# Opening of a residual block kernel on one core: column transposes spread and moved, a third product mixed in, VectorE's angle work and the small loads reordered

## The reference

```python
def rmsnorm(x, gain):
    xf = x.astype(jnp.float32)
    y = xf * lax.rsqrt(jnp.mean(xf * xf, axis=-1, keepdims=True) + RMS_EPS)
    return (y * gain.astype(jnp.float32)).astype(x.dtype)
...
    mod = jax.nn.silu(c) @ w_ada + b_ada
    shift, scale, gate = jnp.split(mod, 3, axis=-1)
    h = rmsnorm(x, norm_pre) * (1.0 + scale[:, None, :]) + shift[:, None, :]
    proj = h @ w_in
    u_pool, z_pool, u_ssm, z_ssm, g_pool, g_ssm = jnp.split(proj, list(IN_SPLITS), axis=-1)
...
    dt = jnp.exp(log_dt.astype(jnp.float32))[:, None]
    lam_re = jnp.minimum(a_re.astype(jnp.float32), -1e-4)
    mag = jnp.exp(lam_re * dt)
    abar_re = mag * jnp.cos(lam_im * dt)
    abar_im = mag * jnp.sin(lam_im * dt)
```

## Time and profile before

| | us |
|---|---|
| median of 3 runs | 974.56 (974.37 to 975.2) |
| the profiled execution, its time | 974.84 |
| the profiled execution, its span in the trace | 973.0 |
| TensorE busy (PE) | 942.2, 97% of the span |
| VectorE busy (DVE) | 650.1, 67% |
| ScalarE busy (ACT) | 345.2, 35% |
| GpSimd busy (POOL) | 46.6, 5% |

### The profile page before, as it was taken

How to read it: one execution, slowest core, us unless ns; L and a number is a source line. 1 busy time by engine, 2 the same in 40 slices (tenths; PEclk the granted TensorE clock), 3 DMA queues, 4 the chain that set the end, 5 groups by cost and what they waited for, 6 DMA issues and landing times.

```text
span 973.0 us, 11601 instructions
## 1 busy us (share of the span) xinstructions
PE 942.2 (97%) x4448; PEld 790.3 (81%) x4448; DVE 650.1 (67%) x912; ACT 345.2 (35%) x401; POOL 46.6 (5%) x82
## 2 busy tenths in 40 slices
PE   0999999999999999999999999999999999999997
PEld 0878888888888888888888888888888888787886
DVE  6968978999888868767887667663344444455233
ACT  6541342322443343644554544631122231133111
POOL 0019800000000000000000000000000000000000
PEclk9999999999999999999999999999999999999999
DMA  9833273544445569667566554897543255322222
GB/s 339 298 113 105 90 262 131 190 155 152 152 160 188 187 204 238 207 180 207 172 187 210 157 155 125 265 334 239 173 154 109 105 201 210 129 87 87 87 87 86
DMA packets 95686, 168.26 MB, mean 173 GB/s; under 512 B 37648, under 2 KB 54160, under 8 KB 95632
## 3 DMA queue, kind: packets, MB, share of 16 engines
q1 hardware_dynamic: 86272, 163.07, 50.1%
q10 hardware_dynamic: 9360, 4.46, 2.1%
HBM read 118.21 MB, written 49.28 MB: 172 GB/s over the span
## 4 chain that ended last, share of the span: by engine, by line
PE 91%; DVE 5%; ACT 2%; DMA 1%; issue 1%; SPq 0%; ACTq 0%; DVEq 0%
PE ps L1791 52%; PE ps L1879 17%; PE ps L1979 8%; PE psb L1879 4%; PE ps L1925 2%; PE psa L1900 1%; PE psa L1848 1%; PE psa L1791 1%; PE psb L1914 1%; PE psb L1912 1%; DMA sin_t<-yp_d 1%; PE psb L1815 1%; DVE mod_out L1268 0%; ACT gt L980 0%; DVE w_lo L1264 0%
## 5 line engine op out<-in xcount | busy, mean ns | idle before, releaser
L1791 PE MATMUL ps<-bop,w_hi 128*128 128x512 f32 x1312 | 352.7, 391 | 0.5 <-DVE bop L1302 0.3
L1791 PEld LDWEIGHTS ps<-bop,w_hi 128*128 128x128 f32 x1312 | 245.2, 188 | 51.6 <-DVE bop L1656 0.6
L1791 PE MATMUL ps<-bop,w_lo 128*128 128x512 f32 x656 | 202.0, 389 | 0.0
L1791 PEld LDWEIGHTS ps<-bop,w_lo 128*128 128x128 f32 x656 | 123.2, 188 | 25.7
L1264 DVE TENSOR_TENSOR w_lo<-raw,w_hi 128x1024 fp32r<-128x1024 f32 x49 | 61.4, 1254 | 59.8 <-ACT w_hi L968 59.7
L968 ACT ACTIVATE w_hi<-raw 128x1024 fp32r<-128x1024 f32 x49 | 51.6, 1057 | 91.8 <-PE ps L1791 84.4
L1879 PE MATMUL ps<-bop,r_hi 128*128 128x512 f32 x208 | 64.1, 390 | 0.0
L1879 PE MATMUL ps<-t_hi,r_hi 128*128 128x512 f32 x140 | 55.2, 395 | 0.0
L1879 PE MATMUL ps<-t_hi,r_lo 128*128 128x512 f32 x140 | 54.6, 390 | 0.0
L1879 PE MATMUL ps<-t_lo,r_hi 128*128 128x512 f32 x140 | 54.5, 389 | 0.0
L1979 PE MATMUL ps<-wo_hi,y_hi 128*128 128x512 f32 x128 | 49.9, 390 | 0.4 <-DVE wo_lo L1721 0.4
(11 more groups left out here) (304 smaller groups left out, 1515.6 us busy)
## 6 DMA issues: line engine op xcount, KB each, us to landing
raw<-in_wstream SPq DMA_DIRECT2D x58, 512.0 KB, 5.4
pair_raw<-in_wstream SPq DMA_DIRECT2D x22, 512.0 KB, 4.7
ada<-in_w_ada SPq DMA_DIRECT2D x16, 512.0 KB, 11.6
x_tok<-in_x SPq DMA_DIRECT2D x8, 512.0 KB, 7.7
gs_d<-gt SPq DMA_DIRECT2D x8, 512.0 KB, 5.0
win_d<-win_new SPq DMA_DIRECT2D x8, 512.0 KB, 4.0
wout_d<-wout_new SPq DMA_DIRECT2D x8, 512.0 KB, 5.6
wout<-wout_d SPq DMA_DIRECT2D x8, 512.0 KB, 4.2
```

The costliest lines, as they stand in the source:

```text
L1791: last = mm(ps[slot(u)][:, f * HALF:f * HALF + HALF], a[:, k, :], b(k, f), start=k == 0 and q == 0, stop=k == KT - 1 and q == 2)
```

## The change

It has four parts, all in the opening.

- **Loads.** ScalarE's queue issues ldt, aim, cols, are and consts; SyncE's starts with x, with c behind tile 3. The first two weight blocks are loaded behind w_ada of k = 0 and k = 1.
- **Row sums.** VectorE takes the squares of tiles 2 and 5 (`square_sum`), ScalarE the other six. `plain_angles` stands ahead of VectorE's first square sum and `reduced_angles` behind it, both ahead of the first scales of x. `sine` and a new function `cosine` (the first part of the old `cos_sin`) move behind the loop over k, ahead of split_lo(3); what is left of `cos_sin` stands behind it. split_lo(0), (1) and (2) stand inside the loop, split_lo(4) moves ahead of `magnitudes`.
- **Transposes.** Columns 0 to 3 are transposed into four PSUM tiles ahead of all products, tokens of the first four x tiles first, as soon as each diagonal exists. ScalarE copies columns 2 to 7 out of PSUM (`xt_out`) and makes h from the copy. Column k + 4 is transposed behind the k steps of k.
- **Third product.** Its k steps stand among those of the first two: k = 0, 1 behind k = 5, then 2, 3 behind 6, the rest behind 7. `split_hi(2)` waits for the last transpose.

```diff
+        xt = [ps[0], ps[1]] + [psb, psa] * 3
...
             for t in range(CH):
                 sp.dma_start(x_tok[:, t, :], x_view[t]).then_inc(tile_in[t], 16)
-            load_w(0)
-            load_w(1)
+                if t == 3:
+                    sp.dma_start(silu_row[:, :], c_d).then_inc(c_in, 16)
             for k in range(KT):
+                if k in (1, 2):
+                    load_w(k - 1)
...
+            act.dma_start(par["ldt"], log_dt_d).then_inc(par_in, 16)
+            act.dma_start(par["aim"], a_im_d).then_inc(par_in, 16)
+            act.dma_start(cols[:, :], cols_d).then_inc(cols_in, 16)
+            act.dma_start(par["are"], a_re_d).then_inc(par_in, 16)
+            act.dma_start(consts[:, :], consts_d).then_inc(small_in, 16)
...
+            def xt_out(k):
+
                 act.wait_ge(xt_done, k + 1)
+                fn(h_full[k][:, :], xt[k][:, :], ACT.Copy).then_inc(xt_taken, 1)
...
+            split_hi(0)
+            h_of(0)
+            h_high(0)
+            xt_out(2)
+            split_hi(1)
+            h_of(1)
+            xt_out(3)
+            h_high(1)
+            for k in range(2, KT):
+                h_of(k)
+                h_high(k)
+                if k + 2 < KT:
+                    xt_out(k + 2)
+                if k == 5:
+                    split_hi(2)
...
+            def square_sum(t):
+                dve.wait_ge(tile_in[t], 16)
+                stt(rt[1][:, :], x_tok[:, t, :], 1.0, x_tok[:, t, :], ALU.mult, ALU.mult,
+                    accum_out=stat[:, 0, t:t + 1]).then_inc(v_sums, 1)
...
                 scale_shift(k)
                 if k:
                     split_h(k - 1)
+                if k < 2:
+                    split_lo(k)
+                if k == 6:
+                    split_lo(2)
             split_h(KT - 1)
-            split_lo(2)
+            sine(steps)
+            cosine(steps)
+            split_lo(3)
             cos_sin(steps)
-            split_lo(3)
+            split_lo(4)
             magnitudes(steps)
             dve.wait_ge(angle_ready, 1)
             factors(steps)
-            split_lo(4)
             complex_factor(steps)
...
+            for tiles in (range(0, 4), range(4, CH)):
+                for k in range(4):
+                    transposed(k, tiles)
+            third = {5: (0, 1), 6: (2, 3), 7: (4, 5, 6, 7)}
             for k in range(KT):
-                if k + 2 < KT:
-                    x_transposed(k + 2)
-                pe.wait_ge(h_done, k + 1)
-                for n in range(2):
-                    last = k_step(("gs", n), k, *h)
-                    if k == KT - 1:
-                        last.then_inc(mm_done, 1)
-            for u in FIRST[2:]:
+                step(0, k)
+                step(1, k)
+                for k3 in third.get(k, ()):
+                    step(2, k3)
+                if k + 4 < KT:
+                    transposed(k + 4, range(CH))
+            for u in FIRST[3:]:
                 product(u, h)
```

More of the change, by code:

```diff
@@ L550, in sine, with cosine @@
             do(stt(wide["sn"], p, 1.0, r, ALU.add, ALU.mult))
-        def cos_sin(steps):
+        def cosine(steps):
             do = steps.do
@@ L568, in cos_sin @@
             do(tt(q, q, p, ALU.mult))
+        def cos_sin(steps):
+            do = steps.do
+            tt = nc.vector.tensor_tensor
+            k, q, z = (wide[m] for m in ("k", "q", "z"))
+            cs, sn = wide["cw"], wide["sw2"]
             do(tt(cs, k, wide["cs"], ALU.mult))
@@ L965, in split_hi @@
                 act.wait_ge(raw_in[p % 2], 16 * (p // 2) + 16)
-                if previous(p) is not None:
+                if p == 2:
+                    act.wait_ge(xt_done, KT)
+                elif previous(p) is not None:
                     act.wait_ge(mm_done, previous(p) + 1)
                 fn((wx_hi if p == 2 else w_hi[p % 2])[:, :, :], raw[p % 2][:, :, :], ACT.Copy).then_inc(hi_done, 1)
[L970 to L976, removed]
-                    act.wait_ge(tile_in[t], 16)
-                    if t:
-                        act.wait_ge(x_sums, t)
-                    fn(gt[t % 2][:, :], x_tok[:, t, :], ACT.Square, accum_out=stat[:, 0, t:t + 1]).then_inc(x_sums, 1)
+            act.dma_start(par["ldt"], log_dt_d).then_inc(par_in, 16)
[3 more added lines that the diff above has]
+            act.dma_start(consts[:, :], consts_d).then_inc(small_in, 16)
+            act.wait_ge(cols_in, 16)
+            fn(stat[:, 5, 0:1], cols[:, 0:1], ACT.Silu)
+            done = 0
+            for half_, tiles in enumerate(X_TILES_ACT):
+                for t in tiles:
+                    act.wait_ge(tile_in[t], 16)
+                    if done:
+                        act.wait_ge(x_sums, done)
+                    fn(gt[done % 2][:, :], x_tok[:, t, :], ACT.Square, accum_out=stat[:, 0, t:t + 1]).then_inc(x_sums, 1)
+                    done += 1
+                if half_ == 0:
+                    act.wait_ge(c_in, 16)
+                    fn(silu_row[:, :], silu_row[:, :], ACT.Silu).then_inc(silu_ready, 1)
                 act.wait_ge(x_var, half_ + 1)
@@ L1282, in _ @@
                 if half_ == 0:
-                    sine(steps)
-            split_lo(0)
-            split_lo(1)
-            dve.wait_ge(silu_ready, 1)
-            do(ts(g_col[:, :], b_ada[:, KT:2 * KT], 1.0, None, ALU.add))
+                    dve.wait_ge(silu_ready, 1)
+                    dve.wait_ge(cols_in, 16)
+                    do(ts(g_col[:, :], b_ada[:, KT:2 * KT], 1.0, None, ALU.add))
             def scale_shift(k):
```

75 lines of the change are left out of this document (46 added, 29 removed).

## The result

The changed kernel took **980.38 us** in the median of five runs (979.11 to 980.92), the kernel before 974.83 in the five beside them (974.37 to 975.37): a ratio of 1.0053, 95% interval 1.0038 to 1.0068. It is slower, where 970.3 was forecast. The profiled execution took 979.22 us (span 977.4).

The account below looks back on a forecast made before the run. TensorE's chain of matmuls was taken to bound the kernel. 1.8 us won at the first product plus 3.0 up to the fourth, less 0.5 of later waits, made 4.3: 974.56 - 4.3 = 970.3 us, range 969.0 to 973.0.

Parts of the forecast that it names:

- Loads: Opening: parameters land and VectorE's first row starts at 5.7 instead of 6.13, lower bound 5.1.
- Rival B: Opening: small loads wait behind rows of x tiles and land at 8 to 9; gain 1.5, time 973.1; chance 12%.
- First scales: Opening: first half ready at 15.9, ScalarE's three squares done at 19.9, Newton and diagonals at 22.0.
- The loop: From the first product to the fourth: 40.24 us instead of 43.24, 3.0 won.
- What comes late: Behind the third product: GpSimd's chain falls back 6.1 us against TensorE; 0.5 lost at the sixth and ninth products.
- factors and powers: VectorE's list ahead of the sixth product's weight residual: 7.8 us, as in the trace before.
- I keep 4.3: The sum: the gain stays 4.3, with nothing deducted for VectorE operations stretched beside GpSimd.
- the wait of 0.3: Before the sixth product: TensorE waits 0.3 us for the residual of its weights.
- the stretch of 2.6: VectorE's list beside GpSimd's further 6.1 us: 2.6 lost if all were stretched, making the gain 1.7 instead of 4.3.
- rival C: Coefficient chain: VectorE's and GpSimd's operations stretch each other by 1 to 3 us; gain 1.3 to 3.3; chance 17%.
- Rival D: First product: clock falls to 1.2 GHz behind TensorE's pause, losing 2.9; gain 1.4, time 973.2; chance 5%.
- rival E: Opening: small loads served behind the x tiles, parameters landing at 14.7; slower than before, 979.3; chance 5%.

Follow-up runs that it names:

- r2: The changed kernel with the three parameters and the columns issued by SyncE ahead of the x tiles; 976.37 us.
- r8: The kernel before with the parameters, columns and constants issued from ScalarE's queue, the rest untouched; 979.10 us.
- r7: r4 with the sixth product's weight residual placed between VectorE's two first powers instead of behind both; 968.88 us.
- r6: The changed kernel with GpSimd's two tables exchanged, so that its operations of 512 elements come last; 977.23 us.
- r9: r4 with three fills of 128x64 put ahead of GpSimd's work; 969.72 us.
- r10: r4 with GpSimd's two tables exchanged, so that its operations of 512 elements come last; 969.23 us.
- r4: The changed kernel with parameters and columns first on SyncE and VectorE's list behind the third product in the order of before; 975.40 us.
- r5: The changed kernel with GpSimd's rotations held until the sixth product's weight residual is done, a diagnosis; 992.2 us in one run.
- r1: The changed kernel with the sixth product's weight residual moved ahead of the complex factor and the powers; 978.74 us.
- r11: r7 with the small loads back in ScalarE's queue as the change has them; 973.72 us.

## Why the prediction was wrong

Two terms of the sum were mis-sized and one was left out. The first pair was forecast at 69.8 + 6 x 10.88 + 0.5 = 135.6 and came at 144.85, 9.3 later: 3.6 at the fourth product (3.5 of it the landing of the parameters), 3.9 more of waiting behind it (the stretch of VectorE's operations beside GpSimd, put at nothing), 1.7 of the lower clock behind that wait. The profiled span came 8.7 above the forecast, 4.4 longer instead of 4.3 shorter.

**Loads: the step failed.** "Above: the small packets now compete with x tiles" was the right worry and 5.7 the wrong choice; VectorE's first row came at 9.24. Rival B had the place and its landing of 8 to 9, with 12%, for which it said the first product would come 2.8 later than forecast; it came 3.5 later, at 33.14. r2 and r8 show it from both sides, 4.0 and 4.6 us. A landing of 3.0 had been carried from a place behind one load of 512 KB (c) to one beside eight x tiles. Rival B's mechanism, a row of an x tile ahead of each row of a small load, fits the landings: with their issues at 0.74 to 2.63 the five small loads land at 4.8, 6.3, 7.8, 9.2 and 10.8, one about every 1.5 us, and at the 398 GB/s that the trace has from 3 to 10 us an x tile of 512 KB and a small load of 32 KB take 1.4. That is an estimate from rates; no run shows the order of the rows. The prediction had the sentence of the Trainium skill, "DMA: Bandwidth & Descriptors", section "Issuing engines are not separate DMA queues", that loads from all engines interleave on the same DMA engines and that issuing elsewhere saves only the issue time. The trace agrees: there was no fast lane, with 7.07 against 3.0, and the forecast should have followed it.

**First scales: right behind their late start.** From VectorE's first row to the first half's scales took 10.1 us (10.2 forecast), to the second half's 4.0 more (4.0), from there to the first product 9.8 (9.7). With the parameters early, in r7 (first row 4.18), the first product is at 28.58, a microsecond better than the 29.6 forecast; of the 1.5 us won at the start 0.5 went to VectorE's wait for x tile 2, which r7 issues 1.85 us later than the changed kernel.

**The loop: right.** 40.24 forecast, 40.29 measured; the stall before the third product is gone.

**What comes late: the dates right, the durations wrong.** GpSimd starts 0.2 us before the third product's end at 73.59, where 0.3 was forecast. The failed step is the 7.8 us of "factors and powers", taken over unchanged, with the stretch by GpSimd's company put at nothing ("I keep 4.3"). It carried a duration to a place where the same operations have other neighbours. The 7.8 became 11.2 and the residual's 1.47 became 1.96; with 0.1 from the factors the residual ended 4.0 us later than said, and the wait of 0.3 became 4.4 (4.0 of lateness, the rest hand-over). The argument with which the stretch of 2.6 was set aside, that GpSimd's 49 us are no longer than before, counted the total; r6, r9 and r10 show that the pairing sets the price, with GpSimd's operations the same (three fills more in r9). The Trainium skill, "SBUF — State Buffer", section "Who interferes with whom", had the exclusion by whole instructions; r4 and r5 agree, with 1.21 against 0.31 us. The estimate of 2.6, made from that company and set aside, was nearer than the nothing that the sum kept. So rival C was the mechanism, at 17%, with 1 to 3 us of stretch where there were 4.0.

**Clock: a term that no case had here.** Rival D put it at the first product at 2.9. There it did not fall in the changed kernel (1.17 behind 2.88 us of idleness), but it did in the profiled runs of r1, r6 and r9, where the fourth product came 41.54 us behind the first instead of 40.3: a price of 1.2, not 2.9. Behind the wait before the sixth product it fell in every profile that had one of 2.1 us or more: the changed kernel, r2, r4 and r6, about 1.7 us each. There a wait of 4.4 costs 6.1.

**Slower: right sign in rival E, wrong way.** Its 979.3 is the nearest of all to the 980.38, by luck: it had all of the loss from parameters that land at 14.7. They came at 9.2, under the 10.0 from which the loads alone make the kernel slower, and the larger part of the loss came from the list. The runs lead from the best kernel to the changed one in two steps: 968.88 (r7) with neither loss, 973.72 (r11) with the loads, 980.38 with both.

## What to carry to other kernels

Where two engines exclude each other, a duration read in company belongs to that meeting and not to the operation: price a moved stretch from its time alone (5.4 here) up to one neighbour's operation for each of its own (15.4), and place what the critical engine waits for so early that this range does not matter, as r7 did for 5.6 us. A load that starts the chain goes first in the queue that would otherwise be filled, not beside it. And a wait of the matmul engine is worth its length plus the slow matmuls behind it.

## What had not been expected of the hardware

- VectorE and GpSimd fall into step: 128x128 operations of 0.28 to 0.32 us each (r5) take 1.14 to 1.31 in r4, begin 0.10 to 0.13 us behind GpSimd's operation of 512 elements and end 0.15 to 0.18 behind it. Whether they do hangs on tenths of a microsecond: with GpSimd 0.6 us later in VectorE's list the same 20 instructions took 9.7 instead of 15.4 us.
- Small loads issued between 0.7 and 2.7 us from ScalarE's queue, beside x tiles, land 4.1, 5.1, 6.1, 7.1 and 8.2 us after their issue, each later than the one before; issued first by SyncE, the three parameters and the columns land after 1.9 to 2.2 us, and VectorE starts at 4.28.
- Behind a pause of 1.9 to 3.3 us ahead of the first product the granted clock fell in three of eleven profiles (pauses of 2.12, 1.90 and 3.31) and stayed up in the others (2.64 to 3.11); the length of the pause does not decide it. What does is open: no run varied what TensorE does ahead of it. Where it fell it cost 1.2 us. Each kernel has one trace, so whether it changes between the runs of one kernel is not shown.
